# Turning expert tokens and outputs with VectorE 32x32 block transposes instead of TensorE

## The reference

```python
def expert_choice_moe(h, router_w, w1, w3, w2):
    cap = CAPACITY_FACTOR * n // N_EXPERTS            # 128 latent rows and 16 prompt rows for each expert
    aff = jax.nn.softmax((xf @ router_w).astype(jnp.float32), axis=-1)
    gate, idx = lax.top_k(aff.T, cap)
    xe = xf[idx]
    a = jnp.einsum("ecd,edf->ecf", xe, w1)
    bg = jnp.einsum("ecd,edf->ecf", xe, w3)
    ye = jnp.einsum("ecf,efd->ecd", jax.nn.silu(a) * bg, w2) * gate[..., None]
    y = jnp.zeros((n, D), h.dtype).at[idx.reshape(-1)].add(ye.reshape(-1, D))
```

## Time and profile before

| | |
|---|---|
| median of 3 runs | 2458.37 us (2457.37 to 2462.35) |
| profiled execution, first to last instruction | 2460.6 us (its own time is not listed apart; the three runs are the ones above) |
| PE busy | 2297.4 us, 93% |
| PE weight loads busy | 1950.2 us, 79% |
| DVE busy | 485.6 us, 20% |
| ACT busy | 350.3 us, 14% |
| POOL busy | 154.8 us, 6% |
| mean granted TensorE clock | 0.963 of full |
| DMA | 530.09 MB, mean 215 GB/s |

### The profile page before, as it was taken

One profiled execution on the slowest core, in us unless ns is written; L12 is line 12 of the kernel. 1 busy time (PEld: TensorE's weight loads), 2 busy tenths in 40 slices (PEclk: granted clock), 3 DMA queues, 4 the chain that ended last, 5 costly groups with the idle time before them and its releaser, 6 DMA issues. The chain is left out here.

```text
span 2460.6 us, 37433 instructions
## 1 busy us (share of the span) xinstructions
PE 2297.4 (93%) x15311; PEld 1950.2 (79%) x15311; DVE 485.6 (20%) x1160; ACT 350.3 (14%) x1005; POOL 154.8 (6%) x184
## 2 busy tenths in 40 slices
PE   8999999885999299999999999999999999999993
PEld 1345555575655199999999999999999999999993
DVE  0111111336885700000000000000001001000002
ACT  0011111231332011111011011111111111111112
POOL 0000000011211000000000000000000000000002
PEclk9899999986999599999999999999999999999996
DMA  9701101216331766886966967969869669679674
GB/s 351 303 30 60 54 36 51 90 53 218 122 135 68 231 213 188 313 270 222 362 213 233 364 207 269 322 213 322 261 226 361 213 233 364 208 277 313 214 262 172
DMA packets 348806, 530.09 MB, mean 215 GB/s; under 512 B 10792, under 2 KB 281936, under 8 KB 347488
## 3 DMA queue, kind: packets, MB, share of 16 engines
q1 hardware_dynamic: 341168, 510.13, 59.7%
q0 software_dynamic: 7600, 19.47, 3.2%
HBM read 493.61 MB, written 35.95 MB: 215 GB/s over the span
## 5 line engine op out<-in xcount | busy, mean ns | idle before, releaser
L1531 PE MATMUL ps_ab<-xeT,ring 128*128 128x144 f32 x8192 | 1010.3, 287 | 2.2 <-DVE xeT L1579 2.2
L1531 PEld LDWEIGHTS ps_ab<-xeT,ring 128*128 128x128 f32 x8192 | 1006.9, 190 | 6.0 <-issue 6.0
L1546 PE MATMUL ps_yy<-hidT,ring 128*128 128x144 f32 x4096 | 505.6, 286 | 0.0
L1546 PEld LDWEIGHTS ps_yy<-hidT,ring 128*128 128x128 f32 x4096 | 502.6, 190 | 2.1
L437 PE MATMUL ps_p<-w_in_sb,hT 128*128 128x512 f32 x720 | 318.6, 596 | 1.6 <-issue 1.6
L1586 DVE TENSOR_TENSOR hidT<-silu,ps_ab 128x144 f32<-128x144 f32 x256 | 77.9, 304 | 929.0 <-ACT silu L1500 914.5
L437 PEld LDWEIGHTS ps_p<-w_in_sb,hT 128*128 128x128 f32 x720 | 135.0, 191 | 155.6 <-issue 155.1
L1500 ACT ACTIVATE silu<-ps_ab 128x144 f32<-128x144 f32 x256 | 74.5, 291 | 933.0 <-PE ps_ab L1531 933.0
L1121 PE MATMUL b_z<-y,mixT 128*128 128x512 f32 x288 | 128.0, 597 | 2.0 <-ACT aff L1057 1.7
L1594 DVE TENSOR_SCALAR ye<-ps_t,slot_gate 128x512 f32<-128x512 f32 x32 | 22.5, 746 | 486.2 <-PE ps_t L1556 486.2
L1477 POOL DMA_INDIRECT stream<-ye,slot_row x16 | 25.8, 1613 | 1361.8 <-DVE ye_p L1596 1361.8
(11 more groups left out here) (256 smaller groups left out, 1199.6 us busy)
## 6 DMA issues: line engine op xcount, KB each, us to landing
ring<-in_exp_w SPq DMA_DIRECT2D x384, 1024.0 KB, 11.6
y<-in_ada_w SPq DMA_DIRECT2D x8, 2048.0 KB, 9.6
w_in_sb<-in_w_in SPq DMA_DIRECT2D x4, 2576.0 KB, 16.3
w_in_sb<-in_ada_w SPq DMA_DIRECT2D x4, 2048.0 KB, 9.6
kv<-kvo SPq DMA_DIRECT2D x15, 512.0 KB, 5.8
kvo<-pr SPq DMA_DIRECT2D x9, 768.0 KB, 3.3
qkT_dram<-qkT SPq DMA_DIRECT2D x9, 512.0 KB, 4.4
qk<-qkT_dram SPq DMA_DIRECT2D x9, 512.0 KB, 5.4
```

Source lines behind the costliest of these rows:

```text
L1531: mm = nc.tensor.matmul(ps_ab[f % 2][:, N * w:N * w + N], unit[:, k, bass.ts(c, P)], xeT[:, k], start=(k == 0), stop=(k == DT - 1))
L1546: mm = nc.tensor.matmul(ps_yy[d % 2][:, 0:N], unit[:, f % 2, bass.ts(d, P)], hT[:, f], start=(f == 0), stop=(f == FT - 1))
```

## The change

The expert block no longer turns anything on PE. DVE's block transpose turns each 32x32 block in place: block row stays block row, so of a [128, 1024] tile every block of 32 partitions and 32 columns is turned and stays where it is. To make that add up to a full turn, the DRAM rows of `normed` and `stream` are stored in another order of columns (four quarters: feature k\*128 + q\*32 + c is stored at q\*256 + k\*32 + c), and each of the 128 slots gathers four quarter rows, one from each of four tokens of a group, with four indirect DMAs; outputs are scattered likewise by four. Prompt pieces keep their one gather and one scatter.

For that order, in `mixing` the residual `x2` is written with strides (`natural`), DVE's `xn2` for PE reads it with strides, and the normed rows for DRAM are a second product, made by POOL from `x2` (`xn2_q`). In `routing` gates and row numbers are spread to four columns. `xeT` has two buffers, the loop runs over pairs of experts, and `finish` undoes the order with four DVE operations for each tile in place of one.

```diff
+def natural(t):
+
+    return t.rearrange("p (q k c) -> p k q c", q=4, c=QUARTER)
+def split(t):
+    return t.rearrange("p (k q c) -> p k q c", q=4, c=QUARTER)
...
@@ mixing, POOL, end of a turn @@
                         nc.gpsimd.tensor_copy(mixT[:, par, HEADS:DT], g.fuT[:, :, bass.ts(i, P)]).then_inc(mix_pool, 1)
+                    if on(i, 2):
+                        pool.wait_ge(rms2_ready, T + 1)
+                        pool.wait_ge(x2_ready, 2 * T + 2)
+                        if not below(i, 3):
+                            pool.wait_ge(normed_stored, 16 * i - 32)
+                        nc.gpsimd.tensor_tensor(xn2_q, x2[:, par], ss[:, 3:4].to_broadcast([P, D]), ALU.mult).then_inc(xn2_q_ready, 1)
...
@@ mixing, DVE @@
-                        did(TS(xn2[:], x2[:, 1 - par], ss[:, 3:4], None, ALU.mult), xn2_ready)
+                        did(TS(split(xn2[:]), natural(x2[:, 1 - par]), ss[:, 3:4], None, ALU.mult), xn2_ready)
-                    did(TT(x2[:, par, cols], x2[:, par, cols], x_in[:, par, cols], ALU.add), x2_ready)
+                    did(TT(half_row, half_row, split(x_in[:, par, cols]), ALU.add), x2_ready)
...
@@ routing, DVE @@
-                did(COPY(at_f[:], at[:]))
-                did(COPY(top_b[:], top[SECOND:HALVES, ::-1]))
-                did(nc.vector.tensor_scalar(at_b[:], ...), picked)
-                did(nc.vector.tensor_scalar(at_f[0:E, :], ...), picked)
+                did(COPY(spread[0][:], fourfold(top[0:E, :])), picked)
+                did(COPY(spread[2][:], fourfold(top[SECOND:HALVES, ::-1])), picked)
+                did(nc.vector.tensor_scalar(spread[1][:], fourfold(at[0:E, :]), float(PROMPT), None, ALU.add), picked)
+                did(nc.vector.tensor_scalar(spread[3][:], fourfold(at[SECOND:HALVES, ::-1]), ..., ALU.add), picked)
...
@@ experts, POOL @@
-                    nc.gpsimd.indirect_dma_start(xe[:], None, g.normed, ...slot_row[:, e:e + 1]...)
+                    for c in range(4):
+                        nc.gpsimd.indirect_dma_start(xe[:, c], None, normed_quarters, ...slot_row[:, c, e:e + 1]...)
-                    nc.gpsimd.indirect_dma_start(g.stream, ...slot_row[:, e:e + 1]..., ye[:], None, compute_op=ALU.add)
+                    for c in range(4):
+                        nc.gpsimd.indirect_dma_start(stream_quarters, ...slot_row[:, c, e:e + 1]..., ye[:, c], None, compute_op=ALU.add)
...
@@ experts, PE: turn_x() and the nine transposes of yT and yT_p are gone @@
-                    pe.wait_ge(gathered, e * 32 + 64)
-                    turn_x()
                     pe.wait_ge(h_kept, e * FT + (FT + 2))
...
@@ experts, DVE @@
+                    nc.vector.transpose(xeS[:]..., xe[:]...).then_inc(xe_turned, 1)
+                    nc.vector.transpose(xeS_p[:]..., xe_p[:]).then_inc(xe_turned, 1)
...
+                def keep_y(e):
+                    dve.wait_ge(yT_kept, e * DT + (DT + 2))
+                    nc.vector.transpose(yS[:]..., yT[:]...).then_inc(y_turned, 1)
+                    nc.vector.transpose(yS_p[:], yT_p[:]...).then_inc(y_turned, 1)
+                    dve.wait_ge(y_turned, e * 2 + 4)
+                    dve.wait_ge(ye_free, e + 1)
+                    for c in range(4):
+                        nc.vector.tensor_scalar(ye[:, c]..., yS[:, :, c], g.slot_gate[:, c, bass.ds(e, 1)], None, ALU.mult).then_inc(ye_kept, 1)
+                    nc.vector.tensor_scalar(ye_p[:], yS_p[:], g.slot_gate_p[:, bass.ds(e, 1)], None, ALU.mult).then_inc(ye_kept, 1)
...
@@ finish, DVE @@
-                    g.dve.did(nc.vector.scalar_tensor_tensor(xs[:, i], xs[:, i], rs[:, i:i + 1], final_g[:], ALU.mult, ALU.mult), scaled)
+                    for q in range(4):
+                        g.dve.did(nc.vector.scalar_tensor_tensor(split(ys[:, i])[:, :, q], natural(xs[:, i])[:, :, q], rs[:, i:i + 1],
+                                                                 split(final_g[:])[:, :, q], ALU.mult, ALU.mult), scaled)
```

More of the change, by code:

```diff
@@ L1505, in _ @@
                         nc.scalar.activation(yT[:, d], ps_yy[d % 2][:, 0:CAP_L], ACT.Copy, scale=g.mod[:, 1, 4, d:d + 1])
-                        nc.scalar.activation(yT_p[:, d], ps_yy[d % 2][:, CAP_L:N], ACT.Copy, scale=g.mod[:, 0, 4, d:d + 1]).then_inc(yT_kept, 1)
+                        nc.scalar.activation(yT_p[:, d % 4, d // 4], ps_yy[d % 2][:, CAP_L:N], ACT.Copy, scale=g.mod[:, 0, 4, d:d + 1]).then_inc(yT_kept, 1)
+                keep_x(0, 0)
+                with act.Fori(0, E // 2 - 1) as j:
+                    for par in range(2):
+                        e = j * 2 + par
+                        gated(e)
+                        keep_x(e + 1, 1 - par)
+                        keep_y(e)
@@ L1508, in _ @@
+                gated(E - 2)
+                keep_x(E - 1, 1)
+                keep_y(E - 2)
+                gated(E - 1)
+                keep_y(E - 1)
             @block.tensor
             def _(pe):
-                def turn_x():
-                    for k in range(DT):
-                        nc.tensor.transpose(ps_t[k // 4][:, bass.ts(k % 4, P)], xe[:, bass.ts(k, P)], g.ident)
-                    nc.tensor.transpose(ps_t[2][:, 0:P], xe_p[:], g.ident).then_inc(xe_turned, 1)
-                pe.wait_ge(gathered, 32)
@@ new lines, in _ @@
+                with pe.Fori(0, E // 2) as j:
+                    for par in range(2):
+                        e = j * 2 + par
+                        pe.wait_ge(xT_act, e + 1)
+                        pe.wait_ge(xT_dve, e + 1)
+                        for f in range(FT):
+                            pe.wait_ge(h_kept, e * FT + (f + 1))
+                            p, c = divmod(f, 2)
+                            for w in range(2):
+                                s, turn = g.slot(2 * p + w)
+                                if c == 0:
+                                    pe.wait_ge(g.slot_loaded[s], e * 32 + 16 * (turn + 1))
+                                unit = g.ring[:, s].rearrange("p (k n) -> p k n", k=DT)
+                                for k in range(DT):
+                                    mm = nc.tensor.matmul(ps_ab[f % 2][:, N * w:N * w + N], unit[:, k, bass.ts(c, P)], xeT[:, par, k],
+                                                          start=(k == 0), stop=(k == DT - 1))
+                            mm.then_inc(ab_summed, 1)
+                        pe.wait_ge(h_kept, e * FT + (FT + 2))
+                        for d in range(DT):
+                            pe.wait_ge(yT_kept, e * DT + (d + 1))
+                            for f in range(FT):
+                                s, turn = g.slot(16 + f // 2)
+                                if d == 0 and f % 2 == 0:
+                                    pe.wait_ge(g.slot_loaded[s], e * 32 + 16 * (turn + 1))
+                                unit = g.ring[:, s].rearrange("p (c n) -> p c n", c=2)
+                                mm = nc.tensor.matmul(ps_yy[d % 2][:, 0:N], unit[:, f % 2, bass.ts(d, P)], hT[:, f], start=(f == 0), stop=(f == FT - 1))
+                                if d == DT - 1 and f % 2 and f < FT - 1:
+                                    mm.then_inc(g.w2_used, 1)
+                            mm.then_inc(y_done, 1)
@@ new lines, in _ @@
+                keep_x(0, 0)
+                with dve.Fori(0, E // 2 - 1) as j:
+                    for par in range(2):
+                        e = j * 2 + par
+                        for f in range(FT):
+                            hidden(e, f)
+                        keep_x(e + 1, 1 - par)
+                        keep_y(e)
+                for f in range(FT):
+                    hidden(E - 2, f)
+                keep_x(E - 1, 1)
+                keep_y(E - 2)
+                for f in range(FT):
+                    hidden(E - 1, f)
```

204 lines of the change are left out of this document (90 added, 114 removed).

## The result

The changed kernel takes 2505.17 us (2503.74 to 2508.72, 4 runs) against 2459.94 us (2457.37 to 2462.35, 4 runs) of the kernel before: ratio 1.0184, 95% interval 1.0171 to 1.0198. The prediction was 2462.1 us, range 2452 to 2472. It was wrong, and the difference of 43 us was in none of its cases.

The account below looks back on a forecast made before the run. PE alone bounds the experts; PE and DVE are nearly full in mixing. -24 + 12.3 + 5.4 + 6.5 + 3.5 = +3.7 us on the profiled span, 2464.3, hence 2462.1 as median; range 2452 to 2472.

Parts of the forecast that it names:

- Experts: what is removed: Expert block: PE transposes go; expert ends gain 24.9 us, taken as -24, and between gate/up and down 0.
- the wait instructions and seven loop branches: PE's expert loop: 0.9 us taken off the 24.9 us gain, as these now have nothing beside them.
- transposes at an expert's end: Expert block: 1.66 us of PE transposes and waiting gone at each of 15 changes of expert, -24 us.
- mixing, seven held turns: Mixing: POOL's new product holds DVE's start of `outputs` in seven turns, 1.75 us each, +12.3 us.
- routing to the first expert: Between routing and first gate/up load: wider DVE operations, more PE transposes and five gathers instead of two, +5.4 us.
- tail: Behind the last expert: DVE's turns and scalings +0.8, five POOL scatters instead of two +5.7; sum +6.5 us.
- finish: Finish: four DVE operations per tile instead of one, 9 tiles, +3.5 us, bounds 1 to 6.
- Gate/up to down: Within an expert: nine transposes go but had covered a wait for DVE; gain 0.0 to 0.2 us, taken as 0.
- The clock rival: Mixing: holds leave PE idle and its clock falls, five turns losing about 2.5 us each, 2475 us; chance 0.1.
- Strided forms: Rival: DVE's strided accesses lose the double rate, finish and wide turn reach upper bounds, 2471 us; chance 0.17.
- POOL slips between the quarters: Finish: lower bound of 1 us, with POOL's power running between DVE's four operations per tile.
- slower: Whole kernel: slower by over 0.2%, above 2463.3 us, from part of the main sum, strided and clock cases; chance 0.45.

Follow-up runs that it names:

- e1: The change with PE's loop back at one expert per pass and one xeT buffer: 2452.06 us, ratio 0.9965 to the kernel before.
- e3: The kernel before with only PE's expert loop changed, to 8 passes of two experts: 2514.73 us, ratio 1.0216.
- e7: The change, two experts per pass, with gate/up sums cut to 5 of 8 feature tiles: 2384.37 us, one execution.
- e8: The kernel before with only PE's expert loop changed, to 4 passes of four experts: 2484.75 us, ratio 1.0097.
- e11: The change, two experts per pass, with gate/up sums cut to 4 of 8 feature tiles: 2376.83 us, one execution.
- e12: The change, two experts per pass, with gate/up sums cut to 3 of 8 feature tiles: 2378.74 us, one execution.
- e2: The change with PE's 16 experts written out in a row, no loop: 2450.58 us, ratio 0.9959 to the kernel before.
- e9: e6 with PE's wait for DVE's last gated products moved into the down group, ahead of the tiles needing them: 2424.74 us, ratio 0.9847.
- e6: e5 with PE's 16 experts written out instead of looped: 2441.11 us, ratio 0.992 to the kernel before.
- e5: e1 with the product of the normed rows moved from POOL to ACT: 2443.65 us, ratio 0.993 to the kernel before.
- e4: e1 with POOL's product of the normed rows cut to one column of 1024: 2441.53 us, ratio 0.9919 to the kernel before.
- e10: e1 with one of four scatters in the last expert and one DVE operation per finish tile: 2448.44 us, ratio 0.9946.

## Why the prediction was wrong, step by step

**The step that failed** is the sentence in "Experts: what is removed": "In the change the next gate/up group follows directly, since its buffers were released long before", and the 0.9 us taken off for "the wait instructions and seven loop branches". It holds inside a pass. At the seven jumps it is wrong: a branch was priced as an instruction with nothing beside it, not as a jump at which PE can stand idle. The diff showed the doubled body, and the change's text names it ("the loop runs over pairs of experts"), but no step asked what a longer body does. By the traces the term is +27.1 us and not -24. e1 gives the transposes alone: 1526.7 - 1551.05 = -24.4. So the term was right to 0.4 us, and the missing one is 7 x 7.36 = 51.5.

What the runs show of it: instruction packets of 16 KB, issue idle before the gate/up matmuls only at jumps back into bodies of two or four experts (4.7 to 6.5 us in the change, e3, e7, e8, e11 and e12), none at jumps back into a body of one (the kernel before, e1), and none in straight-line code (e2, 112 packets).

**The terms**, change against before. The measured ones are read from the two traces unless said otherwise, and add up to the 41.3 us between the spans:

| term | forecast | measured | from |
|---|---|---|---|
| transposes at an expert's end | -24 | -24.4 | e1's expert block |
| jumps of the two-expert body | none | +51.5 | change less e1, expert blocks |
| mixing, seven held turns | +12.3 | +9.7 | rows: 152.3 us before, 162.0 in the change |
| up to routing otherwise | none | -2.3 | rows |
| routing to the first expert | +5.4 | +4.6 | rows |
| tail | +6.5 | +2.0 | rows |
| finish | +3.5 | +0.2 | rows |

*Gate/up to down.* "The gain is 0.0 to 0.2 us; I take 0" was near: 0.91 us of idle stand where 1.16 us of transposes were, and from gate/up to down it is 63.79 us and was 63.89. The 0.1 us, 16 times, are in the -24.4; the 15 expert ends gave 1.54 us each and not 1.66. But the idle time is a term that can be had. e9 shows that without it, and with what else the early start gives, 16 experts are 16 us shorter, which is more than POOL's product cost.

*Mixing.* Routing began 7.4 us later in the change, by the same DVE row before and in the change:

```profile
820.53 0.16 DVE L1386 CAST at_pf<-at_p 16x16 f32<-16x16 uint32 x1
...
827.93 0.16 DVE L1409 CAST at_pf<-at_p 16x16 f32<-16x16 uint32 x1
```

The mechanism is as told: the product takes 1.89 us (forecast 2.1, bounds 1.9 to 2.35), and DVE's two-input `den`, 1.27 us long in place of 0.17, ends with it. Twice the 1.04 us of 512 columns less 1.89 leaves 0.19 for the start-up that was estimated at 0.2. A turn grew by 1.45 us and not by 1.75, mostly because the product is shorter, and seven of them by 9.7. The rest is -2.3: 1.6 us by which mixing had begun earlier, which differs from kernel to kernel (0.1 in e6) and has no cause that was found; 1.6 us won at the router's matmuls, whose clock did not fall (at e5 above); and 0.9 us lost where the last product, taken for 0, held DVE's last `xn2` (1.65 us at 814.64, where it takes 0.75). e5 shows that the hold, and not the work, is the cost: on ACT the same product gives 8.4 us back of the 10.5 that it costs by e4. The clock rival did not come: from 640 to 760 the clock was 1.00 in the change, and at the end it was the clock of before that had been low (0.50 from 804 to 805). Its five turns of 2.5 us each were an estimate that no run shows.

*Routing to the first expert.* The forecast's parts add up to 5.3 and not 5.4. DVE's wide turn took 1.25 us where 1.2 were estimated, and the five gathers came 1.26 apart, as forecast.

*Tail.* POOL's start came 1.1 us later (forecast 0.8) and its issues took 5.55 us longer (5.7). The sum forgot what lies behind them. The last scatter landed 1.80 us after its issue where the old one took 3.46, and from the memset to SP's next load it is 2.76 us and no longer 5.7. The first goes with the size of a wide scatter, 128 KB and no longer 512, and not with their number (e10 has 1.78 with only one of them); that the size is the cause was not tested. For the second no cause was found.

*Finish.* "Bounds 1 (POOL slips between the quarters)" was mostly the case and was taken for the exception; the 0.2 us measured lie below even this bound. DVE and POOL in the change, at the place of the earlier trace rows:

```profile
2482.33 8.02 DVE L1695 SCALAR_TENSOR_TENSOR ys<-xs,rs,final_g_row 128x256 f32<-128x256 f32 x20 [22.10 <-POOL rs L1686]
...
2484.54 0.68 POOL L1686 TENSOR_TENSOR rs<-rs,minus_half 128x1 f32<-128x1 f32 x1
```

20 quarters in 8.02 us are 1.6 us a tile, against 1.73 with one operation. POOL's power, which took 1.49 us beside one long DVE operation, takes 0.68 between short ones. Once, at 2487.85, a small POOL operation took 2.55 us all the same; with the wait behind it the nine tiles take 15.15 us, 1.68 each.

*The rivals.* Strided forms cost nothing: DVE's strided `xn2` takes 0.74 us (748 ns before) and the strided additions 0.69, as the contiguous ones did. Without the doubled body the measured terms add up to -10; e1 gave -9 us, 2452.06, at the lower end of the range. The chances set on "slower" came from cases that did not happen. That the kernel did get slower was luck and bears out none of them.

## What to carry to other kernels

Look at what PE does at the jump back before writing two passes into one. Here a body of one expert (1536 or 1572 loads and matmuls) cost nothing at the jump (e1, the kernel before). One of two experts stood idle for 4.7 to 5.3 us at each jump even at 1792 (e12); with 3072 and more a jump cost 7 to 8 us with the clock's fall (the change, e3, e8). Written out in full, the same code had no such idle time (e2). When work is taken off the busiest engine, look at what it had covered: the 0.9 us wait left behind was hidden by starting the next group's tiles that were ready, and that was worth 16 us where the change with a short body gains 9. Give an added elementwise product to an engine that does not hold its neighbour: beside POOL's product DVE's `den` took 1.27 us, beside ACT's 0.17 (e5).

## What the runs showed of the hardware

- A jump back into a PE body of two or four experts: 4.7 to 5.3 us of idle in the change and its shortened forms (e7, e11, e12), 6.3 to 6.5 in the forms of the kernel before (e3, e8; why 1.4 more stays open), then a granted 0.50, with which an expert's gate/up groups are 1.6 to 3.0 us longer than 62.88 (the change, e3, e8). The page has 86 to 126 instruction packets, against 22 with one expert in the body.
- From 3072 to 2304, 2048 and 1792 loads and matmuls in a body of two experts, eight passes each, 126 packets of 16 KB fall to 102, 94 and 86 (the change, e7, e11, e12): 8 for each 256.
- With PE never idle in the expert block from its first matmul on (e9), an expert takes 94.08 us, 1.0 less than with a wait of 0.72 us in it (e6).
- POOL's product of 128x1024 with a value per row takes 1.89 us (the change), ACT's 1.15 (e5), a DVE turn of 128x1024 fp32 in 32x32 blocks 1.25 (the change).
- Beside POOL's product DVE's `den` took 1.27 us and its last `xn2` 1.65, where they take 0.17 and 0.75 (the change); beside ACT's product `den` took 0.17 (e5).
- A scatter of 128 rows costs POOL 1.57 us with 64 or 128 KB in all (1.87 from start to start, the change) and 1.61 with 512 KB (1.92, the kernel before).
